# The blocks of a pair's second head in the other half of the partitions, in a chunked delta-rule stage

## The chip, the cores and the metric

The kernel runs on one core of one Trainium2 chip. The metric is the device time of one execution in microseconds (us), from the first instruction to the last; the lower the better.

## The reference

The program is three transformer layers over 512 tokens of width 1024, in float32. The change lies in one part of the last layer, the RWKV-7 mixer, whose core is this recurrence (16 heads of 64 features; everything of one head is a 64 x 64 state):

```python
def wkv7_scan(r, w, k, v, a, b):
    def step(state, inp):
        r_t, w_t, k_t, v_t, a_t, b_t = inp
        sa = jnp.einsum('bhij,bhj->bhi', state, a_t)
        state = (state * w_t[:, :, None, :] + sa[..., None] * b_t[:, :, None, :]
                 + v_t[..., None] * k_t[:, :, None, :])
        y_t = jnp.einsum('bhij,bhj->bhi', state, r_t)
        return state, y_t
```

It is called with a = -kk and b = kk * a, where kk is the normed key. The kernel computes it in 8 chunks of 64 tokens: within a chunk the effect of a on b is a strictly triangular 64 x 64 matrix A, and what is needed is X = (I - A)^-1 and a few products with it. Only what leaves a chunk goes through the 8 chunks in order, in a later stage that the change does not touch.

## The kernel before, in words

The features lie on the 128 partitions, so one tile of 128 features is a pair of heads, head 0 in partitions 0 to 63 and head 1 in 64 to 127. A tile is 128 x 512: 512 tokens, or 8 chunks. The stage runs over the m = 0 to 7 head pairs (KD = 8). Each pair has 16 blocks of 64 x 64 (2 heads e, 8 chunks c).

Every product is written by `products`: 16 matmuls of 64 x 64 with 64 moving columns, in float32. In the records one such matmul is two MATMULs and two LDWEIGHTS, so a product is 32 of each. A 64 x 64 matmul uses one quarter of TensorE's array: the half of the rows is given by the partitions of its operands, the half of the columns by the partitions of its output. There are three layouts. By feature, head e is in partition half e. By token and by chunk, the block (e, c) lies in partition half c % 2, whichever the head. A product from features to chunks (the grams `ab_t`, `ab`, `ak_t`, `rk_t`, `rb_t`) or from chunks to features (`r_new`, `y0`, `m`, `n`) therefore meets all four quarters, and its blocks go out in the order QUADRANTS, four quarters in turn, into the two halves of a pair of PSUM banks. A product from chunks to chunks (`z`, `dx`, `dxt`, `u0`, `a_new`, `akv`) has row half = column half = c % 2: it meets only the two quarters on the diagonal, in the order DIAGONAL.

The four token tiles (`b_tok`, `a_tok`, `k_tok`, `v_tok`) are turned by `turned`: four full 128 x 128 transposes or matmuls for each tile, three with "ident" and one (v) with "centre".

For one pair, the inverse is built in five levels n. At each, PE multiplies `z` = lv X, ScalarE copies z out of PSUM, PE multiplies `dx` = Xt z and `dxt` = z Xt, VectorE adds dx into X (`add`) and dxt into Xt (`addt`), and the next level's z waits for the add. lv is the masked A of the level (VectorE, `level`). What does not belong to this chain is put between by hand. PE's queue for pair m is: z1, the end products of the pair before (`ends_x`: u0, a_new), dx1 and dxt1, z2, `ends_r` (r_new, y0), dx2 and dxt2, `ends_m` (m, n), z3, the token tiles of pair m + 1, dx3 and dxt3, `bonus`, `grams_ab`, z4, `grams_k`, dx4 and dxt4, `gram_rb`, z5, `spread` of pair m + 2, `weighted` (akv) of pair m + 1, dx5. VectorE and ScalarE have orders of their own, written in the same way; `need` is a wait on a step of another engine, `mark` the increment that ends a step. The PSUM banks are given by `bank`: z in 0, dx in 1, dxt in 2, the rest share 3 to 7.

```python
        DIAGONAL = [((c + n) % 2, c) for n in range(2) for c in range(NC)]
        QUADRANTS = [(e, c + (e + n) % 2) for c in range(0, NC, 2) for n in range(2) for e in range(2)]
```

## Time and profile before

| | |
|---|---|
| device time, three runs | 3702.94, 3708.01, 3711.56 us; median 3708.01 us |
| the profiled execution: its own time | 3705.42 us |
| its span in the trace | 3703.0 us |
| granted TensorE clock over the span | 0.953 |
| PE busy | 3418.7 us (92%), 22118 matmuls |
| VectorE busy / ScalarE busy | 1870.1 us (51%) / 1174.5 us (32%) |
| HBM read | 279.33 MB, 76 GB/s over the span |

Times in the trace run from the start of the span. PE is the matmul record, PEld the weight load beside it, DVE is VectorE, ACT ScalarE. PEclk is the granted TensorE clock as a share of full speed. L2583 is the matmul in `products`; the whole stage lies between about 2855 and 3118 us. In a timeline row, `x32` is the number of instructions that are merged into the row, the first two numbers are start and duration of the merged row in us, and what stands in square brackets is how long the engine was idle before it and what ended the idle time; "issue" is a wait for nothing that the profile shows.

### The profile page before, as it was taken

The numbers are of one execution on the slowest core, as the hardware profiler recorded it, in microseconds if no ns is written. First come the engines' busy times: TensorE is split into PE (matmuls) and PEld (weight loads), VectorE is DVE, ScalarE is ACT, GpSimd is POOL, SyncE is SP. The second block draws the span as 40 slices with busy tenths as digits, with TensorE's granted clock in tenths as the row PEclk, the third lists the DMA queues.
The fourth block names the chain that finished last, engine by engine and source line by source line (L and its number), as shares of the span: only waits on it lengthen the run. The fifth ranks groups of instructions, "written<-read, shape, count | busy, mean of one in ns | idle before, by whom it ended". The sixth has DMA issues, their size and how long they took to land. (4 is left out here: it accounts for less than half of the span.)

```text
span 3703.0 us, 50171 instructions
## 1 busy us (share of the span) xinstructions
PE 3418.7 (92%) x22118; PEld 2782.0 (75%) x22118; DVE 1870.1 (51%) x2306; ACT 1174.5 (32%) x1444; POOL 76.8 (2%) x52
## 2 busy tenths in 40 slices
PE   8999998999999999698999979999688888799996
PEld 7777787787878888687888857887476777588884
DVE  5344565776354434553544365443744664654435
ACT  3225544322232223242322243221423332232223
POOL 0000000000000001000100020000000000000001
PEclk9899999999999999799999989999698999899998
DMA  4101122222222223122222312222122000122231
GB/s 164 46 35 36 56 103 80 80 100 87 98 84 99 84 99 124 42 86 97 87 95 89 105 57 91 102 86 75 42 73 78 4 4 14 52 91 96 88 108 39
DMA packets 44279, 284.63 MB, mean 77 GB/s; under 512 B 5152, under 2 KB 5408, under 8 KB 17824
## 3 DMA queue, kind: packets, MB, share of 16 engines
q1 hardware_dynamic: 44064, 281.45, 21.9%
q8 instruction: 174, 2.85, 0.3%
q14 instruction: 41, 0.34, 0.0%
HBM read 279.33 MB, written 2.10 MB: 76 GB/s over the span
## 5 line engine op out<-in xcount | busy, mean ns | idle before, releaser
L440 PE MATMUL ps<-xh,wh 128*128 128x512 f32 x2464 | 981.0, 398 | 88.5 <-DVE xl L854 33.9
L440 PE MATMUL ps<-xl,wh 128*128 128x512 f32 x2464 | 971.7, 394 | 0.0
L440 PE MATMUL ps<-xh,wl 128*128 128x512 f32 x2464 | 970.9, 394 | 0.0
L311 DVE TENSOR_TENSOR wl<-raw,wh 128x2048 fp32r<-128x2048 f32 (+3 forms) x284 | 591.4, 2083 | 440.6 <-ACT wh L306 440.2
L440 PEld LDWEIGHTS ps<-xh,wh 128*128 128x128 f32 x2464 | 468.3, 190 | 222.2 <-issue 104.4
L306 ACT CAST wh<-raw 128x2048 fp32r<-128x2048 f32 (+3 forms) x284 | 492.4, 1734 | 301.4 <-PE ps L440 296.0
L440 PEld LDWEIGHTS ps<-xh,wl 128*128 128x128 f32 x2464 | 468.1, 190 | 102.2 <-issue 2.1
L440 PEld LDWEIGHTS ps<-xl,wh 128*128 128x128 f32 x2464 | 468.7, 190 | 98.2 <-issue 2.2
L440 PE MATMUL ps<-hid_h,wh 128*128 128x512 f32 x880 | 346.8, 394 | 2.7 <-DVE wl L311 2.7
L440 PE MATMUL ps<-hid_l,wh 128*128 128x512 f32 x880 | 345.2, 392 | 0.0
L440 PE MATMUL ps<-hid_h,wl 128*128 128x512 f32 x880 | 343.7, 391 | 0.0
L1768 ACT ACTIVATE tmp<-tmp 128x512 f32<-128x512 f32 x88 | 55.7, 633 | 560.7 <-DVE tmp L1776 560.7
L1776 DVE TENSOR_TENSOR tmp<-ps,rs 128x512 f32<-128x512 f32 x88 | 60.9, 692 | 317.4 <-PE ps L440 308.5
L440 PEld LDWEIGHTS ps<-hid_h,wh 128*128 128x128 f32 x880 | 165.7, 188 | 40.3 <-DVE wl L311 4.1
L440 PEld LDWEIGHTS ps<-hid_h,wl 128*128 128x128 f32 x880 | 165.6, 188 | 37.9
L440 PEld LDWEIGHTS ps<-hid_l,wh 128*128 128x128 f32 x880 | 165.6, 188 | 34.6
L2583 PE MATMUL ps<-x_area 64*64 64x64 f32 x4864 | 140.1, 222 | 20.4 <-issue 14.5
L2583 PEld LDWEIGHTS ps<-x_area 64*64 64x64 f32 x4864 | 131.0, 136 | 34.0 <-issue 25.5
L726 POOL TENSOR_TENSOR h<-tmp,h 128x512 f32<-128x512 f32 x48 | 76.6, 1629 | 3553.5 <-DVE tmp L719 3553.5
L1025 DVE COPY ybuf<-ps 128x512 f32<-128x512 f32 x40 | 27.7, 692 | 181.6 <-PE ps L440 181.5
L1056 ACT ACTIVATE tmp<-ybuf 128x512 f32<-128x512 f32 x40 | 25.3, 632 | 285.4 <-DVE ybuf L1025 220.4
L1761 DVE TENSOR_TENSOR hid_l<-tmp,hid_h 128x512 fp32r<-128x512 f32 x110 | 76.1, 692 | 75.5 <-ACT hid_h L1757 75.5
(363 smaller groups left out, 4166.7 us busy)
## 6 DMA issues: line engine op xcount, KB each, us to landing
raw<-in_up SPq DMA_DIRECT2D x88, 1024.0 KB, 4.8
raw<-in_down SPq DMA_DIRECT2D x64, 704.0 KB, 4.0
raw<-in_up_c SPq DMA_DIRECT2D x22, 1024.0 KB, 4.8
raw<-in_down_c SPq DMA_DIRECT2D x16, 704.0 KB, 4.1
raw<-in_gates SPq DMA_DIRECT2D x8, 1024.0 KB, 4.8
raw<-in_gv SPq DMA_DIRECT2D x8, 1024.0 KB, 5.2
raw<-in_gu SPq DMA_DIRECT2D x8, 1024.0 KB, 4.8
raw<-in_gout SPq DMA_DIRECT2D x8, 1024.0 KB, 4.8
```

Of the source, the lines that this page charges most:

```text
L306: nc.scalar.copy(wh[:, slot, 0:w], raw[:, slot, 0:w]).then_inc(hi_ready, 1)
L311: nc.vector.tensor_tensor(wl[:, slot, 0:w], raw[:, slot, 0:w], wh[:, slot, 0:w].bitcast(F32), ALU.subtract).then_inc(lo_ready, 1)
L440: last = nc.tensor.matmul(out, stationary, moving, start=(fresh and q == 0), stop=(t == kt - 1 and half == per - 1 and q == 2), skip_group ...
L726: nc.gpsimd.tensor_tensor(dst, self.scratch(2 + t % 2), dst, ALU.add).then_inc(n_onto.sem, 1)
L1025: last = (nc.vector.tensor_copy(dst, products[m]) if scale is None else nc.vector.tensor_scalar(dst, products[m], scale, None, ALU.mult))
L1056: nc.scalar.activation(squares(u, m), buf[:, k * blocks + m, tokens], ACT.Square).then_inc(act_steps.sem, 1)
L1761: nc.vector.tensor_tensor(hid_l[:, k, tokens], tmp[:, 2 + u, tokens], hid_h[:, k, tokens].bitcast(F32), ALU.subtract).then_inc(dve_steps.s ...
L1768: nc.scalar.activation(tmp[:, u, :], tmp[:, u, :], ACT.Silu).then_inc(act_steps.sem, 1)
L1776: nc.vector.tensor_tensor(tmp[:, u, :], products[0], rs[:, :], ALU.mult).then_inc(dve_steps.sem, 1)
L2583: last = nc.tensor.matmul(dst, stationary, right(rhs, e, c), start=(n == 0), stop=(n == len(pairs) - 1), skip_group_check=True)
```

## The change

Head 1's blocks move to the other partition half in half of the tiles. `rows_of(e, c, turned)` gives the half: c % 2 as before, or (c + e) % 2 for a turned tile. b, k and v tokens, the masked grams, Xt, z and what the ends produce are turned; X, lv and the a tokens are not. Then

- z, dx, u0, a_new and akv each go from one kind to the other, meet all four quarters, and go out in the order QUADRANTS (13 of the 33 products that a pair now has). dxt stays on the diagonal; r_new, y0, m, n and the grams had four quarters before and keep them.
- the token tiles are no longer turned as 128 x 128 but block by block: 16 matmuls of 64 x 64 for each of the four (`token`, and `products` for v).
- Xt needs A in the turned layout, so the gram `ab` is multiplied a second time, `ab_f` (`gram_again`); VectorE masks it straight out of PSUM (`first_xt`) in place of the copy in SBUF.
- outputs lie in halves of bank pairs, z and dx in the two halves of banks 0 and 1, so z1 now also waits for `add5` of the pair before. `bonus` and `spread` share bank 7.
- ScalarE copies b and a tokens in one instruction, k and v in one, and u0 and a_new in one (128 x 1024 each), after the second of the two is done. The token tiles wait for all readers of their bank pair.
- the queues change: akv moves from before z1 to behind z1, `gram_rb` from before z5 to behind it, `gram_again` and `spread` come behind dx5; on VectorE `bonus` goes before the masks, and `scaled_keys` behind the last of them. `ends_x` waits for `xt0` of the next pair in place of `bonus` and `akv` of the next pair.

```diff
-        bank = {"b_tok": 7, "a_tok": 3, "k_tok": 4, "v_tok": 5, "bonus": 7, "ab_t": (3, 0), "ab": (3, 1), "ak_t": (5, 0),
-                "rk_t": (5, 1), "rb_t": (3, 0), "spread": 5, "akv": 6, "u0": 7, "a_new": 6, "r_new": (3, 0), "y0": (3, 1),
-                "m": (5, 0), "n": (5, 1)}
+        bank = {"b_tok": (3, 0), "a_tok": (3, 1), "k_tok": (5, 0), "v_tok": (5, 1), "ab_t": (3, 0), "ab": (3, 1), "ak_t": (5, 0),
+                "rk_t": (5, 1), "rb_t": (3, 0), "ab_f": (5, 0), "akv": (3, 1), "a_new": (5, 0), "u0": (5, 1), "r_new": (3, 0),
+                "y0": (3, 1), "m": (5, 0), "n": (5, 1), "bonus": 7, "spread": 7}
         for n in range(1, 6):
-            bank[f"z{n}"], bank[f"dx{n}"], bank[f"dxt{n}"] = 0, 1, 2
+            bank[f"z{n}"], bank[f"dx{n}"], bank[f"dxt{n}"] = (0, 0), (0, 1), 2
...
+        def rows_of(e, c, turned):
+
+            at_ = C * ((c + e * turned) % 2)
+            return slice(at_, at_ + C)
...
+        def by_turned(x, e, c):
+            o = (e * (NC // 2) + c // 2) * C
+            return x[rows_of(e, c, 1), o:o + C]
...
             def first_xt(m):
-                need(dve, aA, m, "ab")
+                need(dve, pA, m, "ab_f")
                 if m:
                     need(dve, pB, m - 1, "dx5")
-                mark(nc.vector.tensor_tensor(blocks(xt_), blocks(abs_[m % 2]), every(LEVEL), multiply), vB, "xt0")
+                mark(nc.vector.tensor_tensor(of_heads(xt_), in_halves("ab_f"), every_half(LEVEL), multiply), vB, "xt0")
...
-            def end(m, name, out):
-                need(act, pC, m, name)
-                mark(nc.scalar.copy(out, ps[:, bank[name], :]), aC, name)
+            def ends(m):
+                need(act, pC, m, "u0")
+                mark(nc.scalar.copy(tok_pairs["new"][m % 2].rearrange("p q (e s) -> p q e s", e=2), both("a_new")), aC, "new")
...
-            def products(steps, name, out, *pairs):
+            def products(steps, name, out, *pairs, order=QUADRANTS):
 
-                for e, c in (QUADRANTS if out in (half_chunk, half_feature) else DIAGONAL):
+                for e, c in order:
...
+            def token(name, x, out):
+                for e, c in QUADRANTS:
+                    last = nc.tensor.matmul(out(name, e, c), by_feature(x, e, c), of_head(table("ident"), e, c), start=True,
+                                            stop=True, skip_group_check=True)
                 mark(last, pA, name)
...
+            def gram_again(m):
+                need(pe, vA, m, "rk_t")
+                gram("ab_f", t_a, t_b)
+
             def weighted(m):
-                need(pe, vA, m, "rk_t")
-                products(pA, "akv", whole_token, (by_chunk, ak_ts[m % 2], by_token, v_toks[m % 2]))
+                need(pe, vA, m, "rb_t")
+                products(pA, "akv", half_chunk, (by_turned, ak_ts[m % 2], by_turned, v_toks[m % 2]))
 
             def z(m, n):
                 if n == 1:
                     need(pe, vA, m, "lv1")
+                    if m:
+                        need(pe, vB, m - 1, "add5")
                 else:
                     need(pe, vB, m, f"add{n - 1}")
-                chunk_product(f"z{n}", lv_, xs_[m % 2])
+                products(pB, f"z{n}", half_turned, (by_chunk, lv_, by_chunk, xs_[m % 2]))
...
-                chunk_product(f"dx{n}", xt_, z_)
+                products(pB, f"dx{n}", half_chunk, (by_turned, xt_, by_turned, z_))
                 if n < 5:
-                    chunk_product(f"dxt{n}", z_, xt_)
+                    products(pB, f"dxt{n}", whole_turned, (by_turned, z_, by_turned, xt_), order=DIAGONAL)
 
             def ends_x(m):
                 need(pe, vB, m, "add5")
+                need(pe, aA, m, "akv")
                 if m + 1 < KD:
-                    need(pe, vA, m + 1, "bonus")
-                    need(pe, aA, m + 1, "akv")
-                else:
-                    need(pe, aA, m, "akv")
-                products(pC, "u0", whole_token, (by_chunk, xs_[m % 2], by_token, ak_ts[m % 2]))
-                products(pC, "a_new", whole_token, (by_chunk, xs_[m % 2], by_token, a_toks[m % 2]))
+                    need(pe, vB, m + 1, "xt0")
+                products(pC, "a_new", half_turned, (by_chunk, xs_[m % 2], by_chunk, a_toks[m % 2]))
+                products(pC, "u0", half_turned, (by_chunk, xs_[m % 2], by_chunk, ak_ts[m % 2]))
...
             for m in range(KD):
                 behind, ahead, next_ = m > 0, m + 1 < KD, m + 2 < KD
                 z(m, 1)
+                weighted(m)
                 if behind:
                     ends_x(m - 1)
                 dx(m, 1)
...
                 dx(m, 4)
+                z(m, 5)
                 if ahead:
                     gram_rb(m + 1)
-                z(m, 5)
+                dx(m, 5)
+                if ahead:
+                    gram_again(m + 1)
                 if next_:
                     spread(m + 2)
-                if ahead:
-                    weighted(m + 1)
-                dx(m, 5)
```

## Rows read from the trace of the kernel before

**Rows 1.** The page: PE over the span, and the queue that carries PE's instructions

```profile
PE 3418.7 (92%) x22118; PEld 2782.0 (75%) x22118; DVE 1870.1 (51%) x2306; ACT 1174.5 (32%) x1444; POOL 76.8 (2%) x52
...
q8 instruction: 174, 2.85, 0.3%
```

**Rows 2.** Windows: us, then PE, PEld, DVE, ACT, POOL busy, PEclk, DMA, GB/s

```profile
2868.00:2898.00 30.00, 24.48 (x664) 22.05 (x664) 19.89 (x32) 10.09 (x21) 0.00 (x0) 0.89 0.01 3
2898.00:3056.00 158.00, 137.06 (x4600) 124.00 (x4600) 108.73 (x171) 54.39 (x100) 0.00 (x0) 1.00 0.02 4
3056.00:3086.00 30.00, 26.47 (x921) 24.53 (x918) 20.34 (x33) 8.64 (x16) 0.00 (x0) 1.00 0.02 4
3086.00:3118.00 32.00, 23.92 (x928) 22.82 (x928) 13.42 (x21) 6.84 (x12) 0.00 (x0) 1.00 0.02 4
```

**Rows 3.** Timeline of PE: the `spread` behind pairs 0 and 5

```profile
2893.85 1.12 PE L2618 MATMUL ps<-key_norms,const 32*128 32x512 f32 x2 [1.19 <-DVE spare_l L2385]
...
3052.00 1.12 PE L2618 MATMUL ps<-key_norms,const 32*128 32x512 f32 x2 [1.18 <-DVE x_area L2385]
```

**Rows 4.** Timeline, the bare chain of the last pair: dx3, add3, z4, copy, dx4

```profile
3100.13 2.08 PE L2583 MATMUL ps<-x_area 64*64 64x64 f32 x64 [0.68 <-ACT x_area L2517]
...
3101.33 0.69 DVE L2375 TENSOR_TENSOR spare_l<-ps,spare_l 128x512 f32<-128x512 f32 x1 [0.54 <-PE ps L2583]
...
3102.07 1.15 PE L2583 MATMUL ps<-spare_l,x_area 64*64 64x64 f32 x32
...
3103.27 0.59 ACT L2517 COPY x_area<-ps 128x512 f32<-128x512 f32 x1 [1.85 <-PE ps L2583]
...
3103.91 2.08 PE L2583 MATMUL ps<-x_area 64*64 64x64 f32 x64 [0.69 <-ACT x_area L2517]
```

**Rows 5.** Timeline of PE: bonus and two grams; b, a, k tokens; v tokens

```profile
2979.98 1.12 PE L2647 MATMUL ps<-rs,const 128*128 128x512 f32 x2
2981.03 1.16 PE L2583 MATMUL ps<-x_area 64*64 64x64 f32 x64
...
2974.72 1.53 PE L2609 MATMUL ps<-const,x_area 128*128 128x128 f32 x12
...
2976.90 1.13 PE L2611 MATMUL ps<-const,v 128*128 128x128 f32 x8 [0.66 <-ACT ag L2529]
```

**Rows 6.** Timeline of PE: between two stalls in pair 3

```profile
2969.58 3.01 PE L2583 MATMUL ps<-x_area 64*64 64x64 f32 x128 [0.91 <-issue]
2973.34 0.51 PE L2583 MATMUL ps<-x_area 64*64 64x64 f32 x19 [0.75 <-issue]
```

**Rows 7.** DMA from 2970 to 2974 us, in slices of 0.1 us

```profile
GB/s 0 0 0 0 0 0 164 0 0 0 0 0 0 0 0 0 0 0 0 0 0 0 0 0 0 0 0 0 0 0 0 0 0 0 0 0 0 0 0 0
...
q8 instruction: 1, 0.02, 2.0%
```

**Rows 8.** DMA of the whole stage, 2860 to 3118 us

```profile
q8 instruction: 57, 0.93, 1.6%
```

**Rows 9.** What PE waited for, 2868 to 3118 us: us, times, longest

```profile
PE ps L2583 <- issue: 20.0, 25, 1.5
PE ps L2611 <- ACT ag L2529: 3.4, 6, 0.7
```

**Rows 10.** Timeline of the turn of pair 2 to 3: add5, mask, bonus, ends

```profile
2959.88 0.69 DVE L2375 TENSOR_TENSOR x_area<-ps,x_area 128x512 f32<-128x512 f32 x1 [2.64 <-PE ps L2583]
2960.49 0.68 DVE L2385 TENSOR_TENSOR spare_l<-ps,masks 128x512 f32<-128x512 f32 x1
...
2961.09 0.68 DVE L2389 TENSOR_TENSOR v<-ps,v 128x512 f32<-128x512 f32 x1
...
2961.87 1.32 PE L2583 MATMUL ps<-x_area 64*64 64x64 f32 x38 [1.10 <-issue]
```

**Rows 11.** Windows and PE's timeline where the granted clock is half

```profile
2870.40:2877.20 6.80, 5.38 (x96) 5.22 (x96) 4.48 (x8) 0.58 (x1) 0.00 (x0) 0.50 0.02 4
...
2871.19 5.38 PE L2583 MATMUL ps<-x_area 64*64 64x64 f32 x96 [3.25 <-DVE x_area L2370]
```

More of the change, by code:

```diff
@@ L2211, in rwkv @@
         abs_ = (ab, ab_other)
[L2212 removed]
+        b_toks, a_toks, ak_ts, rk_ts, k_toks, v_toks, rb_ts, xs_ = zip(*sets)
+        tok_pairs = {"b_a": (x_area[:, 8:10, :], spare_h[:, 0:2, :]), "new": (x_area[:, 9:11, :], spare_h[:, 1:3, :]),
+                     "k_v": (x_area[:, 12:14, :], spare_l[:, 0:2, :])}
         reset, masks = area("reset", [P, T], 92 * KB), area("masks", [P, 11, C], 94 * KB)
@@ L2319, in operand_a @@
                 if m:
-                    need(dve, pA, m - 1, "ak_t")
+                    need(dve, pA, m - 1, "ab_f")
                 by, of = blocks(e_kk), blocks(t_a)
@@ L2331, in operand_b @@
                 if m:
-                    need(dve, pA, m - 1, "rb_t")
+                    need(dve, pA, m - 1, "ab_f")
                 mark(nc.vector.tensor_tensor(t_b, e_kk, e_wi, multiply), vL, "b")
@@ L2344, in first_x @@
                 if m >= 2:
-                    need(dve, pC, m - 2, "a_new")
+                    need(dve, pC, m - 2, "u0")
                 x = xs_[m % 2]
@@ L2373, in add_x @@
                 need(dve, pB, m, f"dx{n}")
-                x = xs_[m % 2]
-                mark(nc.vector.tensor_tensor(x, ps[:, bank[f"dx{n}"], :], x, add), vB, f"add{n}")
+                x = in_heads(xs_[m % 2])
+                mark(nc.vector.tensor_tensor(x, in_halves(f"dx{n}", False), x, add), vB, f"add{n}")
             def add_xt(m, n):
@@ L2416, in grams @@
                 with_eye(m)
+                bonus(m)
                 masked(m, "ak_t", ak_ts[m % 2], STRICT, "rk_t")
@@ L2420, in grams @@
                 masked(m, "rb_t", rb_ts[m % 2], UPTO, "rb_t")
-                bonus(m)
             masks_here(dve)
@@ L2493, in decays, with tokens @@
                 mark(nc.scalar.activation(tile(wc, m), e_w[:, C - 1:T:C], ACT.Copy), aE, "wc")
-            def token(m, name, out):
-                need(act, pA, m, name)
+            def tokens(m, name, behind):
+                need(act, pA, m, behind)
                 if m >= 2:
                     need(act, pC, m - 2, "n")
-                mark(nc.scalar.copy(out, ps[:, bank[name], :]), aA, name)
+                out = tok_pairs[name][m % 2].rearrange("p q (e s) -> p q e s", e=2)
+                mark(nc.scalar.copy(out, both("b_tok" if name == "b_a" else "k_tok")), aA, name)
             def lower(m):
@@ L2508, in weighted @@
                 need(act, pA, m, "akv")
-                mark(nc.scalar.copy(ak_ts[m % 2], ps[:, bank["akv"], :]), aA, "akv")
+                mark(nc.scalar.copy(in_heads(ak_ts[m % 2]), in_halves("akv", False)), aA, "akv")
             def z(m, n):
@@ L2549, in _ @@
                 z(m, 1)
+                weighted(m)
                 if behind:
-                    end(m - 1, "u0", ak_ts[(m - 1) % 2])
-                    end(m - 1, "a_new", a_toks[(m - 1) % 2])
+                    ends(m - 1)
                 z(m, 2)
@@ L2559, in _ @@
                 if ahead:
-                    tokens(m + 1)
+                    tokens(m + 1, "b_a", "a_tok")
+                    tokens(m + 1, "k_v", "v_tok")
                 z(m, 4)
@@ L2568, in _ @@
                     decays(m + 2)
-                if ahead:
-                    weighted(m + 1)
-            end(KD - 1, "u0", ak_ts[(KD - 1) % 2])
-            end(KD - 1, "a_new", a_toks[(KD - 1) % 2])
+            ends(KD - 1)
             answer(KD - 1)
@@ L2615, in spread @@
                 if m:
-                    need(pe, vA, m - 1, "rk_t")
+                    need(pe, vA, m - 1, "bonus")
                 rows = slice(32 * (m % 4), 32 * (m % 4) + 32)
@@ L2693, in ends_x @@
-                products(pC, "u0", whole_token, (by_chunk, xs_[m % 2], by_token, ak_ts[m % 2]))
-                products(pC, "a_new", whole_token, (by_chunk, xs_[m % 2], by_token, a_toks[m % 2]))
-            def ends_r(m):
-                need(pe, aC, m, "a_new")
-                if m + 1 < KD:
-                    need(pe, vA, m + 1, "rb_t")
-                products(pC, "r_new", half_feature, (by_token, a_toks[m % 2], by_chunk, rb_ts[m % 2]))
-                products(pC, "y0", half_feature, (by_token, ak_ts[m % 2], by_chunk, rb_ts[m % 2]),
-                         (by_token, v_toks[m % 2], by_chunk, rk_ts[m % 2]))
@@ new lines, in ends_x, with ends_r @@
+                products(pC, "u0", half_turned, (by_chunk, xs_[m % 2], by_chunk, ak_ts[m % 2]))
+            def ends_r(m):
+                need(pe, aC, m, "new")
+                if m + 1 < KD:
+                    need(pe, aA, m + 1, "akv")
+                products(pC, "r_new", half_feature, (by_turned, a_toks[m % 2], by_turned, rb_ts[m % 2]))
+                products(pC, "y0", half_feature, (by_turned, ak_ts[m % 2], by_turned, rb_ts[m % 2]),
+                         (by_turned, v_toks[m % 2], by_turned, rk_ts[m % 2]))
@@ L2724, in _ @@
             gram_rb(0)
+            gram_again(0)
             spread(1)
-            weighted(0)
             for m in range(KD):
```

117 lines of the change are left out of this document (47 added, 70 removed).

## The prediction

> **What bounds the kernel now.** I read the page first: PE 92% busy, the other engines far below [rows 1]. Only the stage of the head pairs changes, so I went on to the windows of that stage. Pairs 1 to 5 issue 4600 matmuls in 158 us, 920 a pair, and PE counts as busy for 137 of them, VectorE for 109, ScalarE for 54 [rows 2]. The spread, once a pair, gives the period: (3052.00 - 2893.85) / 5 = 31.63 us [rows 3]. The stage ends in the states that the next one begins with, so what it gains or loses the kernel does too.
>
> Then the timeline, for what a product costs. On two quarters, 64 matmuls (dx and dxt) take 2.08 us [rows 4]; the last 0.22 us of a row is the modelled end of the last matmul, so that is 0.93 us a product, 29 ns a matmul. On four quarters, 64 matmuls of two grams take 1.16 us [rows 5], 0.47 us a product, 14.6 ns a matmul. So a product of two quarters that moves to four is done in 0.46 us less. The bare chain runs dx3, add, z4, copy, dx4 in 3.78 us a level [rows 4].
>
> Last, PE's idle time. 20.0 us in the stage, 25 times, are put down to "issue" [rows 9]. The stall at 2973.34 begins in the middle of a product, where the code waits for nothing. Between the end of the stall before it and this one lie exactly 128 matmuls, with their loads 256 instructions [rows 6]. The queue q8 carries PE's instructions: 44236 matmuls and loads on 174 packets are 254 a packet [rows 1]. The packet between the two stalls starts at 2970.6, 1.0 us after PE went on at 2969.58, takes 2.0% of 16 x 4 us = 1.3 us, and PE goes on 1.4 us after its end [rows 6, 7]. So I read: when PE enters a block of 256 instructions, the next one is asked for, and it is there 1.0 us, the packet and 1.4 us later. Over the stage a packet takes 1.6% x 16 x 258 / 57 = 1.16 us [rows 8]. **No 256 instructions can then go by in less than about 3.6 us**, which is 28 ns a matmul with its load: hardly less than what a product on two quarters takes anyway, and twice what one on four takes.
>
> The Trainium skill, "Runtime: NRT & Kernel Launch", section "Instruction fetch mechanics", says that instructions come in blocks of 16 KiB (256 instructions) fetched while the current one runs, and that the cost of crossing into the next is mostly hidden. The trace agrees with the block and differs on the cost.
>
> **The change, part by part.**
> 1. z, dx, u0, a_new and akv, 13 products: 13 x 0.46 = 6.0 us of matmul time less a pair.
> 2. `ab_f`: 0.47 us and 32 matmuls more.
> 3. Token tiles: 12 + 8 matmuls in 1.53 + 1.13 us [rows 5], about 2.2 us without the tails, become 4 x 32 matmuls in 4 x 0.47 = 1.9 us: no gain worth the name, but 108 matmuls more.
> 4. Together 6 us less to do, in 920 - 20 + 32 + 128 = 1060 matmuls: 2120 instructions and some 35 waits, 2155 for 256 a block, 8.4 blocks. At 3.6 us they take **30.3 us**. Before, 1840 + 35 are 7.3 blocks, 26.4 us, under a period of 31.63: the supply only showed as single stalls. After, it sets the pace.
> 5. Waits. I walked the new queues through one pair as if instructions were always there, with 0.47 and 0.93 us for products, 0.27 us from the start of a product's last matmul to its reader (z4's at 3102.07 + 1.15 - 0.22 = 3103.00, the copy at 3103.27 [rows 4]), 0.6 us from one VectorE start to the next [rows 10], 0.69 and 0.59 us for an add and a copy [rows 4], 1.0 us for a copy of 1024 (an estimate, twice the 0.59 less its fixed part), 1.1 us for bonus and for spread [rows 3, 5]. A whole pair comes to about 25 us. The slow place is its turn. From the end of dx4, VectorE does add4, addt4, bonus, two masks and lv1 before add5 (ends at 4.9 us), then the rb mask, k2, rkr and xt0 (ends at 7.4), for which `ends_x` waits; `gram_again` waits for the rk mask (3.75), spread ends at 5.3, a_new can start at 7.45 and dx1 at 8.4 us. That lies beside 290 matmuls, 8.3 us of supply: they cover each other but for some 0.3 us.
> 6. Tokens wait for y0, n and their banks: 2.3 us from dxt2's or z3's end, beside 64 to 128 matmuls (1.8 to 3.6 us of supply), hidden but for a few tenths at worst. The larger ScalarE copies lie beside PE work. ScalarE and VectorE get no more to do.
> 7. Removed: `ends_x` no longer waits for `bonus`, which ends at 2961.77 and lets PE idle 1.1 us [rows 10]; the wait for `xt0` (point 5) takes its place. The v tokens' wait for n, 3.4 us in the stage [rows 9], becomes that of point 6. In the new pace both are time in which the next block arrives.
>
> **The sum.** Pairs 1 to 5: 30.3 + 0.3 = 30.6 against 31.6, 5 x 1.0 = 5 us less. Pair 6: no spread, 30.3 against 29.7 (its z1 to the next): 0.6 us more. Pair 0 has no ends, 804 matmuls or 23 us of supply, and took 30 us, at half clock for 6.8 us of them, when 96 matmuls on two quarters took 5.4 us [rows 11]; there the chain sets the time. dx1 to dx3 becomes about 2.5 us shorter (z2, dx2, z3 and the tokens' order), dx3 to the next z1 1.1 us (452 matmuls of supply, 12.9 us, against 14.0), the start 0.5 us (two grams wait for two copies, not four): 4 us less. The last pair: up to dx3, 512 matmuls of supply, 14.6 us against 15.5: 0.7 less. From there five products at 0.46 on the bare chain [rows 4] and u0 and a_new, 3.2 us, less 0.4 for the copy of both: 3 us less, since 448 matmuls of supply (12.8 us) still go under 13 of 16. Sum: -5 + 0.6 - 4 - 0.7 - 3 = -12 us. The profiled execution took 3705.4 us, the median of the runs shown is 2.6 us above it: 3708.0 - 12 = 3696. Small losses where supply and chain fall out of step are likelier than further gains, so I say **3697 us**, its own range 3690 to 3704.
>
> **The rivals.**
> - *The supply is no limit* (0.06). Then the walk of point 5 holds: 25 us a pair against 31.6 is 5 x 6.6 us, some 5 more in pair 6 and 14 in the first and last together, 52 us: 3656 us. This is what the page named above would make of it. Against it stand the stall in mid-product [rows 6] and 25 waits for "issue" [rows 9].
> - *No measurable change* (0.23). Supply and chain don't overlap at the turn of a pair: a block that arrives late there delays addt4 and with it the VectorE row up to xt0. At 1 us a pair the gain of pairs 1 to 5 is gone, 3701 us; if the same happens in pairs 0, 6 and 7, up to 3709 us. For it speaks that at the turn both need 8.3 us, so each slip adds.
> - *Slower, the four quarters do not run side by side* (0.07). In the new z, dx, r_new, y0, m and n, the two row halves write into the same bank of the pair at the same time; in today's four-quarter products each row half keeps its bank. If that costs them the pace, all 33 products take 0.93 us: 30.7 + 2.2 + the waits of the turn, about 35.5 us a pair, +3.9 x 7: 3735 us. It decides only from about 25 ns a matmul, since up to there the supply is slower. Against it: today's two-quarter products have both row halves in one bank and run at 58 ns for each quarter, as the four-quarter ones do (4 x 14.6). The Trainium skill, "TensorEngine Tiling (Array Packing)", section "Restrictions and Gotchas", says that different row tiles cannot access one PSUM bank at the same time. By that rule this rival would hold; the trace of the diagonal does not show it.
> - *Slower, the clock* (0.04). PE now works in bursts with stalls between. If the granted clock fell to half for half of the stage, as in [rows 11], where matmuls took twice as long, a pair would take about 39 us (29 products at 0.93, dxt at 1.87, bonus and spread at 2.2): +7 x 4 = 28 us: 3736 us. Against it: 1.00 from 2898 on, through stalls of over 1 us [rows 2, 6].
> - *The forecast* has the rest, 0.60.
>
> A measurement of this kernel can tell about 0.2%, 7.4 us, from no change. Of the forecast's 0.60 some 0.54 lies below 3700.6: with the first rival, faster 0.60. Within 0.2%: 0.06 + 0.22 = 0.28. Slower: 0.11 and 0.01 of the second rival, 0.12. The range leaves out the first rival and the two slow ones: 3686 (nothing lost anywhere, all 67 blocks of the stage at 3.6 us: 242 us against 262) to 3709.
>
> **What would show it.** Right: q8 packets in the stage up from 57 to about 66, one every 3.6 us; most of PE's idle time put down to "issue", far over 20 us; z and dx as rows of 32 in 0.47 + 0.22 us where no stall cuts them; a spread every 30.6 us; VectorE and ScalarE as busy as before; clock 1.00. Wrong: a period of 27 us or less (supply no limit), matmuls of z at 29 ns (quarters), waits of PE on VectorE over 1 us a pair at `ends_x` (turn), PEclk under 1 in pairs 1 to 6.

## The result, and the profile after

| | before | after |
|---|---|---|
| median of 20 runs | 3705.97 us (3702.13 to 3712.06) | **3719.19 us** (3704.45 to 3729.52) |
| mean granted clock over those runs | 0.951 | 0.9465 |
| the profiled execution: its own time, span, clock | 3705.42, 3703.0 us, 0.953 | 3710.82, 3708.4 us, 0.949 |

The changed kernel takes 1.0031 of the time of before (95% interval 1.0021 to 1.0040): some 11.5 us slower, where 12 us faster was forecast. (The ratio goes by the means, 3706.90 and 3718.31 us; the medians are 13.2 us apart.) The profiled execution of after is one of its quicker ones, so the profile shows less than half of the difference: something varies from run to run.

The page of after, PE over the span and its instruction queue, which answers to [rows 1]:

```profile
PE 3407.5 (92%) x23238; PEld 2769.5 (75%) x23238; DVE 1869.7 (50%) x2306; ACT 1172.0 (32%) x1420; POOL 76.8 (2%) x52
...
q8 instruction: 183, 3.00, 0.3%
```

There are 1120 more matmuls and nine more packets of instructions, as the change asks for; yet PE is busy for 11 us less, and the kernel is slower.

Windows of after, one for each head pair (columns as in [rows 2]):

```profile
2863.00:2893.00 30.00, 25.91 (x826) 23.55 (x824) 20.68 (x34) 9.26 (x17) 0.00 (x0) 0.73 0.02 4
2893.00:2925.00 32.00, 24.99 (x1065) 21.98 (x1060) 21.63 (x34) 10.61 (x17) 0.00 (x0) 1.00 0.02 4
2925.00:2957.00 32.00, 26.21 (x1060) 23.44 (x1051) 21.63 (x35) 10.61 (x17) 0.00 (x0) 0.95 0.02 4
2957.00:2994.00 37.00, 29.12 (x1070) 25.60 (x1063) 21.56 (x35) 10.67 (x17) 0.00 (x0) 0.86 0.02 4
2994.00:3025.00 31.00, 24.66 (x1059) 21.84 (x1055) 21.43 (x35) 10.60 (x17) 0.00 (x0) 1.00 0.02 5
3025.00:3058.00 33.00, 26.71 (x1087) 23.96 (x1088) 22.47 (x36) 10.61 (x17) 0.00 (x0) 0.95 0.02 4
3058.00:3092.00 34.00, 26.97 (x1072) 24.38 (x1074) 19.86 (x33) 8.25 (x12) 0.00 (x0) 0.90 0.02 4
3092.00:3122.00 30.00, 22.29 (x943) 20.95 (x939) 11.69 (x18) 7.17 (x11) 0.00 (x0) 0.94 0.02 4
```

The column to read is PEclk. Before, it stood at 1.00 from 2898 us on [rows 2]; now six of eight windows are below it. Added up over the clock's records from the first `z1` to the last `n`, the granted clock was half for 43.6 us, against 6.8 us before [rows 11]. Some 16 us of the 43.6 lie in pair 0, in one stretch of 17.1 us that begins at 2862.0. Where the clock stayed full, in pairs 1 and 4, a pair takes 32.1 and 31.2 us. That is no less than before and 0.6 to 1.5 us more than forecast. From the end of one pair's `z1` to the end of the next one's, in us:

| | 0 | 1 | 2 | 3 | 4 | 5 | 6 | 7 | stage | at half clock |
|---|---|---|---|---|---|---|---|---|---|---|
| before | 30.0 | 31.1 | 31.8 | 31.8 | 31.3 | 32.2 | 29.7 | 31.6 | 249.4 | 6.8 |
| after | 29.9 | 32.1 | 32.4 | 36.9 | 31.2 | 33.1 | 33.4 | 30.5 | 259.5 | 43.6 |
| e1, below | 27.1 | 30.7 | 31.6 | 31.3 | 30.7 | 33.2 | 29.9 | 27.9 | 242.4 | 19.7 |

The last row is of e1, the first experiment below. So there are two things to explain: why a pair at full clock gained nothing, and why the clock fell.

**A product at one quarter's pace.** VectorE's adds show how far `dx` and `dxt` of one level end apart. The timeline of VectorE in after, add3 (L2391) and addt3 (L2395) of pair 4:

```profile
3012.34 0.69 DVE L2391 TENSOR_TENSOR x_area<-ps,x_area 128x512 f32<-128x512 f32 x1 [2.85 <-PE ps L2591]
3013.90 0.69 DVE L2395 TENSOR_TENSOR x_area<-ps,x_area 128x512 f32<-128x512 f32 x1 [0.87 <-PE ps L2591]
```

They start 1.56 us apart; the working had 0.93 us for `dxt`. By PE's own records it is 1.64 us in the median, 32 matmuls at 51 ns. The reason can be read in the code. DIAGONAL takes e = (c + n) % 2. The blocks of the second head now lie turned, in row half (c + e) % 2, and for e = (c + n) % 2 that is n for every c. The output lies in the same half, so the first eight blocks all use one quarter of the array, and the other eight use another. Two quarters are used, but one after the other. (The matmuls of a product with both row halves in one bank do keep the four-quarter pace: a_new and u0 below.)

Timeline of PE in after, a_new and u0, and the b and a tokens:

```profile
2995.85 1.16 PE L2591 MATMUL ps<-spare_h,spare_l 64*64 64x64 f32 x64 [1.04 <-DVE x_area L2384]
...
3007.95 1.15 PE L2615 MATMUL ps<-const,x_area 64*64 64x64 f32 x64
```

64 matmuls in 1.16 us are 0.47 us a product, as the two grams of [rows 5]. The four quarters do run side by side.

**Instructions.** Timeline of PE in after, last pair, three stalls in a row:

```profile
3098.75 2.71 PE L2591 MATMUL ps<-x_area 64*64 64x64 f32 x128 [0.83 <-issue]
3102.37 2.36 PE L2591 MATMUL ps<-x_area 64*64 64x64 f32 x107 [0.91 <-issue]
3105.84 0.46 PE L2591 MATMUL ps<-spare_l,x_area 64*64 64x64 f32 x15 [0.75 <-issue]
```

PE goes on at 3098.75, 3102.37 and 3105.84, 3.62 and 3.47 us apart, and the first of these stretches is exactly 128 matmuls: 256 instructions with their loads. This is the supply of [rows 6]. One thing has to be added to the working. In after's stage no instruction packet on q8 starts sooner than 3.28 us behind the one before it, and in the stage of none of the other profiles is that distance under 3.2 us. But 128 matmuls in a row that begin in the middle of a block can be quicker: at full clock, two of pair 1's grams and what follows them in pair 0's queue do it in 2.10 us, the last one's end included:

```profile
2882.71 2.10 PE L2591 MATMUL ps<-x_area 64*64 64x64 f32 x128
```

So the limit is from one block to the next; a stretch that begins in the middle of a block isn't bound by it. The DMA of the stage in after (2863 to 3122 us), and what PE waited for in it:

```profile
q8 instruction: 63, 1.03, 1.7%
```

```profile
PE ps L2591 <- issue: 27.7, 29, 2.2
PE ps L2591 <- DVE x_area L2384: 5.2, 6, 1.0
PE ps L2615 <- ACT ag L2545: 4.7, 4, 1.2
```

63 packets in 259 us are one every 4.1 us. The supply limits in places, but over the stage it is not used up: the waits for `xt0` (L2384), which sit at `ends_x` of six pairs, and the slow `dxt` (e13 below) leave it idle.

**The clock.** Windows of after, before and behind one of the falls, and PE's timeline there:

```profile
2974.70:2978.10 3.40, 1.21 (x82) 1.06 (x75) 0.00 (x0) 1.83 (x2) 0.00 (x0) 0.99 0.02 5
2978.10:2984.90 6.80, 6.80 (x95) 5.18 (x98) 2.61 (x3) 0.00 (x0) 0.00 (x0) 0.50 0.01 2
```

```profile
2974.82 0.68 PE L2591 MATMUL ps<-const,v 64*64 64x64 f32 x32
2975.29 0.56 PE L2591 MATMUL ps<-x_area 64*64 64x64 f32 x23
2978.04 3.52 PE L2591 MATMUL ps<-x_area 64*64 64x64 f32 x41 [2.19 <-issue]
2981.49 2.07 PE L2645 MATMUL ps<-rs,const 128*128 128x512 f32 x2
```

PE had 1.21 us of work in the 3.4 us before 2978.10, with a stall of 2.19 us in the middle of a product. Behind it the clock is at half, 1.2 GHz, for 6.8 us, in which 95 matmuls keep PE busy without a gap and `bonus` takes 2.07 us instead of 1.12. The falls in the stage don't all look like this one. There are eight, and the longest idle time of PE in the 5 us before each was, in order:

| fall at, us | 2862.0 | 2926.9 | 2964.4 | 2978.1 | 3036.1 | 3063.4 | 3080.5 | 3118.0 |
|---|---|---|---|---|---|---|---|---|
| idle before, us | 1.1 | 1.0 | 2.2 | 2.2 | 1.6 | 1.9 | 1.9 | 1.1 |
| then at half clock, us | 17.1 | 3.4 | 3.4 | 6.8 | 3.4 | 3.4 | 3.4 | 3.4 |

No single stall of a given length goes with a fall. In e1's profile a stall of 1.85 us at 3028.1 is followed by 19 us at full clock. Before `spread`, PE waits 1.2 us for VectorE in the kernel before, six times, and the clock stays full (two of them in [rows 3]); behind the same wait it fell three times in the profiled execution of e12, four times in e2 and three times in e3 (the experiments below). What decides it is not shown here.

### The profile page after: what moved, and what is told of

Same layout as the page of the kernel before. It is cut to its first block and busy times, and to the rows that moved or that the text cites. A ratio compares the mean times of both kernels' runs of the same rounds, so it can differ in the third digit from the quotient of the medians.

```text
span 3708.4 us, 52376 instructions
## 1 busy us (share of the span) xinstructions
PE 3407.5 (92%) x23238; PEld 2769.5 (75%) x23238; DVE 1869.7 (50%) x2306; ACT 1172.0 (32%) x1420; POOL 76.8 (2%) x52
## 5 line engine op out<-in xcount | busy, mean ns | idle before, releaser
L1025 DVE COPY ybuf<-ps 128x512 f32<-128x512 f32 x40 | 27.7, 692 | 179.9 <-PE ps L440 179.8
```

The lines of the kernel that those rows point to most:

```text
L1025: last = (nc.vector.tensor_copy(dst, products[m]) if scale is None else nc.vector.tensor_scalar(dst, products[m], scale, None, ALU.mult))
```

## The experiments

Ratios are to runs of the kernel before that were taken beside the experiment's, with their 95% interval; where two experiments are compared, it is by these ratios. "Clock" is the mean granted clock of a kernel's runs.

### e1: the order of dxt alone

```
+        BY_HEAD = [(e, c) for e in range(2) for c in range(NC)]
...
-    products(pB, f"dxt{n}", whole_turned, (by_turned, z_, by_turned, xt_), order=DIAGONAL)
+    products(pB, f"dxt{n}", whole_turned, (by_turned, z_, by_turned, xt_), order=BY_HEAD)
```

> The changed kernel with one thing altered: dxt goes out head by head, so that its 16 blocks alternate between the two diagonal quarters; in the changed kernel the order DIAGONAL with turned blocks sends eight in a row to one quarter (1.64 us a dxt in its trace, against 0.93 before). Theory A (the order of dxt is the loss, and the half-clock windows follow from work on one quarter): dxt back to 0.93 us, no more half-clock windows inside the stage than before, a pair about 30.6 us, device time some 10 us under the kernel before. Rival B (the clock falls because PE works in bursts between instruction stalls): dxt at 0.93 us, but the granted clock still falls to half several times in the stage and the time stays within 5 us of the changed kernel. Rival C (the supply of instructions hides dxt's order): no change of the period at full clock, 31.2 us.

Measured: 3700.94 us, **0.9989 (0.9977 to 1.0001)**, clock 0.950. VectorE in e1, add3 and addt3 of one pair:

```profile
3007.82 0.69 DVE L2392 TENSOR_TENSOR x_area<-ps,x_area 128x512 f32<-128x512 f32 x1 [2.85 <-PE ps L2592]
3008.76 0.69 DVE L2396 TENSOR_TENSOR x_area<-ps,x_area 128x512 f32<-128x512 f32 x1 [0.24 <-PE ps L2592]
```

0.94 us apart. Windows of e1 (pair 2, most of pair 4, pair 5):

```profile
2927.00:2958.00 31.00, 22.83 (x1056) 19.67 (x1047) 22.18 (x35) 10.61 (x17) 0.00 (x0) 1.00 0.02 4
2990.00:3020.00 30.00, 21.82 (x1025) 19.07 (x1020) 21.20 (x34) 10.53 (x17) 0.00 (x0) 1.00 0.02 4
3020.00:3054.00 34.00, 25.47 (x1108) 21.78 (x1112) 24.44 (x39) 10.68 (x18) 0.00 (x0) 0.93 0.02 5
```

Its instruction packets and PE's waits for "issue" in the stage:

```profile
q8 instruction: 64, 1.05, 1.8%
```

```profile
PE ps L2592 <- issue: 40.0, 36, 2.2
```

One line of issue order is worth 0.42% between after and e1, 16 us. Of pairs 1 to 5, those at full clock throughout are 4 with 30.7 us and 2 with 31.6 (forecast 30.6); a packet comes every 3.8 us, and 40 us of idle time go to "issue". With the order that the forecast had assumed, the forecast's picture is there in the main, but its 12 us are not: 4 us, with no change at the edge of the interval. The stage of the profiled run is 7 us shorter than before. Neither theory A nor rival B holds as it was put down. `dxt` is back at 0.93 us, but the clock still falls four times, 19.7 us of the stage against 6.8 before; and the time is 16 us under after's, not within 5. Rival C falls by the time; the few pairs at full clock (30.7 and 31.6 us, in after 31.2 and 32.1) would not have decided it.

### e2: the kernel before with dxt on one quarter at a time

```
+        BY_HALF = [(e, c) for h in range(2) for e in range(2) for c in range(h, NC, 2)]
...
-                    chunk_product(f"dxt{n}", z_, xt_)
+                    products(pB, f"dxt{n}", whole_chunk, (by_chunk, z_, by_chunk, xt_), order=BY_HALF)
```

> The kernel before with dxt alone in the changed kernel's order: the eight blocks of one partition half, then the eight of the other. Theory A: dxt 1.64 us in place of 0.93, z behind it late by about 0.6 us four times a pair, some 15 to 20 us more in all, and half-clock windows in the stage if one quarter at work is what lowers the clock. Rival B: +15 us at the most from the products themselves and the clock stays at 1.00 in pairs 1 to 6, since the supply of instructions is as slack as before.

Measured: 3730.93 us, **1.0058 (1.0044 to 1.0071)**, clock 0.950. `dxt` takes 1.68 us; four in a pair are 4 x 0.75 x 8 = 24 us more, and 21.5 came. The clock has a share in this: it is 0.950 against 0.9515 for before, and in the profiled execution it falls to half four times between 2900 and 3037 us, each time behind the wait for VectorE before `spread`. At equal clock (below) some 18 us are left. So in the kernel before, `dxt` lies on the path with about three quarters of its length.

### e8, e13: two quarters again, with dxt in either order

e8 is e1 with z, dx, akv, a_new and u0 head by head, which was meant to let two quarters run side by side, not four; e13 is e8 with dxt in DIAGONAL again.

```
-                products(pB, f"z{n}", half_turned, (by_chunk, lv_, by_chunk, xs_[m % 2]))
+                products(pB, f"z{n}", half_turned, (by_chunk, lv_, by_chunk, xs_[m % 2]), order=BY_HEAD)
...
```

> The kernel with dxt alternating, and z, dx, u0, a_new and akv (13 products a pair) in the order head by head, which uses two quarters at a time: everything of the new layout is kept, only the four quarters are given up. Each of the 13 takes 0.93 us again, 6.0 us more matmul time a pair. If the supply of instructions sets the pace (3.6 us for 128 matmuls, 28 ns each, hardly less than the 29 of two quarters): 0.5 to 1.5 us a pair, 3705 to 3713 us, and the clock lowered less often, since PE works more evenly. If PE's own time or the chain sets it: 4 to 6 us a pair, 3730 to 3750 us.

> The changed kernel with its 13 four-quarter products in the order head by head (two quarters at a time) and dxt as in the changed kernel (one quarter at a time): the fourth of a square whose others are the changed kernel, dxt alternating, and two quarters with dxt alternating. If dxt's order costs the same with and without the four quarters: 3719 to 3722 us. If the four quarters are what lowers the clock, since PE then stands idle between blocks: less than the changed kernel, 3712 to 3717 us, with a mean granted clock above its 0.9465.

Measured, e8: 3703.34 us, **0.9992 (0.9979 to 1.0006)**, clock 0.952. e13: 3707.17 us, **0.9995 (0.9985 to 1.0006)**, clock 0.951. Together with after and e1 this is a square:

| | dxt on one quarter | dxt on two |
|---|---|---|
| 13 products on four quarters | 1.0031 (after) | 0.9989 (e1) |
| 13 products on two quarters | 0.9995 (e13) | 0.9992 (e8) |

The label "two quarters" is only nearly right. Head by head, these products meet two quarters with their first eight blocks and the other two with the last eight, and the halves overlap. Timeline of PE in e13, dx5 of the last pair:

```profile
3113.01 0.97 PE L2592 MATMUL ps<-x_area 64*64 64x64 f32 x32 [0.69 <-ACT x_area L2534]
```

Without the 0.22 us at its end that is 0.76 us, where a product in the kernel before takes 0.93 [rows 4]; two in a row (z1 and akv, a_new and u0) take 1.35 us in both e8 and e13. So the 13 products cost 0.2 to 0.3 us each, 2.6 to 3.6 us a pair and 21 to 29 us in all, and not the 48 us of the expectation.

The lower row of the table: with the products on two quarters dxt's order costs 1 us, which is within the intervals, and the upper row: with four it costs 16 us. Read by columns: the four quarters, which do these 21 to 29 us less of matmul time, give 1 us in the one case and take 13 us in the other. Where they went shows in the stages of the profiled executions. From e1 (2868.16 to 3111.54 us) to e8 (2868.97 to 3116.82) PE's busy time is up from 179.5 to 196.9 us, and its idle time down from 63.8 to 50.9: three quarters of the additional busy time went into time in which PE had stood idle. Timeline of PE in e8:

```profile
3033.26 2.78 PE L2592 MATMUL ps<-x_area 64*64 64x64 f32 x128 [1.11 <-issue]
3036.73 0.57 PE L2592 MATMUL ps<-x_area 64*64 64x64 f32 x19 [0.69 <-issue]
```

Even here PE goes on at 3033.26 and 3036.73, 3.47 us apart.

In e13 the same goes for `dxt`. PE's waits for "issue", in e8 and then in e13:

```profile
PE ps L2592 <- issue: 30.6, 34, 1.7
```

```profile
PE ps L2592 <- issue: 14.4, 18, 1.5
```

The slower `dxt` has filled 16 us of the time in which the next block was on its way. In e2 it filled less: "issue" is 10.7 us there, against 20.0 in before [rows 9], and `dxt` cost 18 to 21 us. This fits, but no run tests it; the turned kernel has another order of tokens and ends as well. And it doesn't say why the same order costs 16 us with the four quarters, where the profiles have even more idle time. The mean clocks do differ there: 0.9465 (after) and 0.9498 (e1) with four quarters, 0.9509 (e13) and 0.9518 (e8) with two. Both orders of `dxt` have the lower clock with four quarters, and four quarters with `dxt` on one have by far the lowest.

### e3, e4: more matmuls in the kernel before

```
             def gram(name, left, right):
+                if name in ('ab_t', 'ab', 'ak_t', 'rk_t'):
+                    for e, c in QUADRANTS:
+                        nc.tensor.matmul(half_chunk(name, e, c), by_feature(left, e, c), by_feature(right, e, c), start=True,
+                                         stop=True, skip_group_check=True)
```

e4 repeats only ab_t and ak_t, and takes the added ones in DIAGONAL.

> The kernel before with four grams (ab_t, ab, ak_t, rk_t) issued twice in the order of the four quarters: 128 matmuls a pair more, 1.9 us of PE time, one block of 256 instructions. By the supply of instructions (3.6 us for 256): 8.3 blocks a pair, 30 us at least, and more stalls: 2.5 to 3.5 us a pair, 20 to 28 us in all, and clearly more than the run with two grams twice. If the supply is no limit: 1.9 us a pair at most, 15 us, and the same as that run.

> The kernel before with two grams (ab_t, ak_t) issued twice, the added ones on two quarters at a time: 64 matmuls a pair more, 1.9 us of PE time as in the run with four grams twice, but half a block of instructions. By the supply: 28 us a pair, so still under the period, and only the PE time counts: about 12 to 15 us in all. If the supply is no limit: the same as the run with four grams twice.

Measured, e3: 3736.62 us, **1.0075 (1.0062 to 1.0089)**, clock 0.952. e4: 3717.07 us, **1.0029 (1.0015 to 1.0043)**, clock 0.952. In e3 the added matmuls would take 4 x 0.47 = 1.9 us a pair at their pace, 15 us in all; 0.75% are 28 us, 3.5 us a pair. That is what one block of 256 instructions costs at the pace of the stalls (3.5 to 3.6 us). e4 was meant to add the same matmul time, but it doesn't: its added products overlap their halves too, and ab_t's takes 0.70 us in e4's trace (from the first matmul to the next product's), not 0.93. So e4 adds about 1.4 us a pair, 11 us, and cost 11 us: its matmul time and no more. With 64 more matmuls a pair, e3 costs 13 us more than its matmul time. That speaks for a price of the instructions themselves, without any quarter being changed. The profiled execution of e3 shows only part of it as idle time: the stage (2865.23 to 3140.71 us) is 24.0 us longer than before's (2865.85 to 3117.31), with PE busy for 18.4 us more and idle for 5.7 us more, and some 7 us more of it are at half clock.

### e6: e1 without the second gram

```
             def gram_again(m):
-                gram("ab_f", t_a, t_b)
+                e, c = QUADRANTS[-1]
+                mark(nc.tensor.matmul(half_turned("ab_f", e, c), by_feature(t_a, e, c), by_feature(t_b, e, c), start=True,
+                                      stop=True, skip_group_check=True), pA, "ab_f")
...
-  mark(nc.vector.tensor_tensor(of_heads(xt_), in_halves("ab_f"), every_half(LEVEL), multiply), vB, "xt0")
+  mark(nc.vector.tensor_tensor(blocks(xt_), blocks(abs_[m % 2]), every(LEVEL), multiply), vB, "xt0")
```

> The kernel with dxt alternating, and the second gram (ab_f) left out but for its last block, so that 30 matmuls a pair fall away; Xt is masked from the copy of ab in SBUF, so the blocks of head 1 in it are in the wrong half and the output is not the reference's. By the supply of instructions: 60 instructions fewer, 8.2 blocks a pair, 29.5 us, 0.8 us a pair or about 6 us under the kernel with dxt alternating (3700.9), and fewer half-clock windows. If the supply is no limit and the chain at the turn of a pair sets the time: nothing or 0.5 us a pair at most.

Measured: 3703.76 us, **0.9995 (0.9985 to 1.0006)**, clock 0.948. 30 matmul records less a pair (60 of 2155 instructions, a quarter of a block) gave nothing that is measured. "Fewer half-clock windows" was wrong: the granted clock is lower than e1's, and in the profiled execution about 41 us of the stage are at half, against e1's 19.7. Its time at equal clock is in the account below.

### e9: fewer instructions, but mixed shapes

e1 with the first head's token tiles as four matmuls of 64x128, beside eight of 64x64 for the second head: 44 calls a pair for the four token tiles instead of 64, each call two matmul records:

```
+                for n in range(TB):
+                    last = nc.tensor.matmul(ps[:, b, o:o + HD], x[0:HD, n * P:(n + 1) * P], of_head(onto, 0, 0), start=True, ...)
+                    if turned:
+                        for c in (2 * n, 2 * n + 1):
+                            last = nc.tensor.matmul(half_turned(name, 1, c), by_feature(x, 1, c), of_head(onto, 1, c), start=True, ...)
```

> The kernel with dxt alternating, and the token tiles made with fewer matmuls where the layout allows it: two chunks of a head in one matmul of 128 stationary columns for head 0 of all four tiles and head 1 of a; 44 matmuls in place of 64, so 40 recorded matmuls or 80 instructions a pair fewer, 0.3 block. By the supply: 1.1 us a pair, some 8 us under the kernel with dxt alternating, 3693 us, and the best version so far. If the supply is no limit: within 2 us of it, or slower by what the mixed shapes cost.

Measured: 3773.46 us, **1.0182 (1.0164 to 1.0200)**, clock 0.940. Timeline of PE in e9, the b tokens at full clock:

```profile
3012.67 0.43 PE L2621 MATMUL ps<-const,x_area 64*128 64x64 f32 x2
3013.03 0.33 PE L2625 MATMUL ps<-const,x_area 64*64 64x64 f32 x4
3013.29 0.43 PE L2621 MATMUL ps<-const,x_area 64*128 64x64 f32 x2
```

Six records take 3013.29 - 3012.67 = 0.62 us, against 6 x 14.6 ns = 0.09 us for 64x64 alone; with two changes of shape in each group some 0.2 us a change remain, an estimate (the wider matmul's own time is not known). Three tiles with eight changes each are 24 x 0.2 = 5 us a pair, 38 us in all; the rest of the 72 us above e1 comes with a clock lower by 0.010. The stage has eight falls in e9's profile. Before most of them PE counts as busy without a gap, but with few matmuls, here before a fall and behind it (columns as in [rows 2]):

```profile
2940.20:2943.61 3.41, 3.41 (x43) 2.87 (x44) 0.00 (x0) 1.01 (x1) 0.00 (x0) 1.00 0.03 7
2943.61:2950.44 6.83, 6.83 (x93) 5.89 (x92) 0.69 (x1) 1.01 (x1) 0.00 (x0) 0.50 0.00 0
```

So the clock falls without any stall as well. Nothing about the supply can be learnt from e9, since the shapes cost more.

### e10, e11, e12: room on PE, and the turn of the pair

e10 is e1, and e11 the kernel before, with `bonus` issued three times (4 matmuls of 128x512 and some 2.1 us of PE time more in each pair, 8 instructions):

```
+                for _ in range(2):
+                    nc.tensor.matmul(ps[:, bank["bonus"], :], table("heads"), e_sum, start=True, stop=True)
```

e12 is the kernel before with another order of VectorE's queue: `bonus` ahead of the masks of the grams, `scaled_keys` behind the last mask.

```
+                    bonus(m + 1)
                     masked(m + 1, "ak_t", ak_ts[(m + 1) % 2], STRICT, "rk_t")
...
                     masked(m + 1, "rb_t", rb_ts[(m + 1) % 2], UPTO, "rb_t")
-                    bonus(m + 1)
                 if next_:
+                    scaled_keys(m + 2)
                     bonus_terms(m + 2)
```

> The kernel with dxt alternating, and the bonus matmul (128x512, all of the array) issued three times in place of once, with the same result: 2.1 us more PE time a pair, but 8 instructions. If the supply of instructions sets the pace, PE has room: under 0.7 us a pair, within 5 us of the kernel with dxt alternating (3701), and, if the clock falls because PE has too little to do between blocks of instructions, a higher mean granted clock than its 0.950 and then even no more time. If PE's time or the chain sets it: 2 us a pair, 15 us more.

> The kernel before with the same two added matmuls of 128x512 a pair. Its period of 31.6 us is not set by the supply (26.4 us) but by PE's queue with its waits: 1.5 to 2.1 us a pair, 11 to 16 us more. If its PE had as much room as the supply theory says of the changed kernel: nothing.

> The kernel before with one part of the change alone: VectorE's queue of the changed kernel at the turn of a pair (bonus ahead of the masks, scaled keys behind them), so that the end products no longer wait for the bonus (1.1 us a pair). Layout, products and instructions as before. The supply allows 26.4 us a pair, so the wait is really gained: 0.7 to 1.1 us a pair, 5 to 8 us in all, 3698 to 3702 us, as good as the changed kernel with dxt alternating. Rival: the stall only moves to the next block of instructions or to xt, and nothing is gained.

Measured, e10: 3708.25 us, **1.0002 (0.9992 to 1.0011)**, clock 0.951. e11: 3727.19 us, **1.0044 (1.0028 to 1.0060)**, clock 0.951. e12: 3705.55 us, **0.9991 (0.9980 to 1.0001)**, clock 0.951. The same 17 us of PE time with hardly an instruction in it cost the kernel before 16 us, nearly all, and e1 about 5 us (1.0002 against 0.9989). In e1, PE time between dxt3 and the grams is largely covered; before, it is on the path. Part of e10's small price is the clock, as its expectation had it: 0.951 against e1's 0.950, and in the profiled execution one fall behind pair 0 where e1 has three. At equal clock (below) the 17 us cost 8 us. e12 missed its 5 to 8 us. It shows that the part of the change that has nothing to do with quarters, `ends_x` no longer behind `bonus`, can be had alone, and its ratio stands where e1's does. What PE waited for in the stage of e12:

```profile
PE ps L2582 <- issue: 9.5, 19, 1.1
PE ps L2582 <- DVE x_area L2370: 7.9, 7, 1.3
```

"Issue" is down from 20.0 us [rows 9], and waiting for VectorE at L2370, one wait of 3.3 us before, is up to 7.9: most of the gain went there, as the rival had it. Neither e1 nor e12 is shown to beat the kernel before: both intervals reach 1.0001.

### The time at equal clock

The runs of one kernel differ in granted clock, and their times follow it. After's run at 0.950 took 3704.45 us and one at 0.944 took 3729.52. The clock is on record to 0.001 only, so what follows is rough. A straight line through the runs of each kernel in the table falls by 1.7 to 3.4 us for 0.001 of clock, and gives at 0.950:

| | before | after | e1 | e8 | e13 | e6 |
|---|---|---|---|---|---|---|
| mean clock | 0.951 to 0.952 | 0.9465 | 0.9498 | 0.9518 | 0.9509 | 0.9479 |
| us at 0.950 | 3711 to 3712 | 3706 | 3703 | 3709 | 3710 | 3701 |

At equal clock after is 5 us quicker than before, e1 8 us, e6 11 us, and the four quarters bring 6 us with dxt on two quarters and 4 us with dxt on one. At the clock that each kernel is granted nothing of that is left. Measured from before to after: -5 at equal clock, then 0.005 of clock at about 3 us for 0.001, +15; the sum, +10, is near the 11.5 us measured. The same way e2 comes to 3729 and e10 to 3711. This is an account from many runs and not an experiment, for no kernel here changed the clock alone.

## Why the prediction was wrong

- **The step that failed, first: point 5's 0.93 us for `dxt`.** That price is one of two quarters side by side. The order DIAGONAL on turned blocks takes them one behind the other, 1.64 us. The row halves of `by_turned` and DIAGONAL both stood in the diff; I carried the price over from [rows 4] by the name of the order, and never listed which quarter each of the 16 blocks falls on. e1 shows this to be 16 us of the 24 between the forecast's -12 and the measured +11.5. How the 16 us come about is only in part known. The longer `dxt` alone is about 0.7 us, 32 times, or 21 us. With the products on two quarters the same order costs 1 us (e13 against e8), so it is the order together with the four quarters that costs. By the account at equal clock e1 and after are 3 us apart and the rest goes with the clock; in the profiled stages, 17.1 us apart, after has 23.9 us more at half clock, which is worth 12 us at the most.
- **The step that failed, second: the rival of the clock at 0.04**, with "1.00 from 2898 on, through stalls of over 1 us" against it. It is what happened, though not at the rival's size: not half of the stage, but 43.6 us of 259.5 at half, 36.8 us more than before. At twice the time for what ran there, that is worth at most 18 us, and about 15 by the account at equal clock, where the rival had 28. The argument against it was drawn from one execution. The kernel before has the same clock of 1.00 behind waits of 1.2 us there, but in its variants e2, e3 and e12 the clock fell behind the same waits. With four quarters the mean clock is lower (0.9465 against 0.9509 and, hardly clear of the spread between runs, 0.9498 against 0.9518); that this comes of PE having less to do between blocks is only argued. For it speak the fall behind 2.2 us of stall and that e10, with more work for PE, has a slightly higher clock than e1. But e1 has more "issue" than after (40.0 against 27.7 us) and the higher clock, so idle time alone does not explain after's, and the cause stays open. I had counted "late instructions" and "clock" as two cases with separate chances; here both came together.
- **Point 4, the supply: right as a lower bound, its period a little short.** Stalls 3.5 to 3.6 us apart, 128 matmuls between them; 63 packets where about 66 were forecast; 21 to 29 us of matmul time removed by the four quarters bring 1 us (e8 against e1); e3 costs 13 us more than its matmul time. But the pairs at full clock take 30.7, 31.2, 31.6 and 32.1 us in e1 and after, 0.1 to 1.5 us over the 30.6, so the 0.3 us for the waits at the turn was too little. The Trainium skill, "Runtime: NRT & Kernel Launch", section "Instruction fetch mechanics", has this crossing as mostly hidden. For matmuls as short as these the measurements decide against it: 40.0 us in e1's stage in 36 waits, 1.1 us a time and 2.2 at the longest.
- **Points 1 and 3, the pace of four quarters: right.** 64 matmuls in 1.16 and 1.15 us. So the rival that the four quarters do not run side by side falls. The Trainium skill, "TensorEngine Tiling (Array Packing)", section "Restrictions and Gotchas", forbids two row tiles one PSUM bank at a time; a_new and u0 have both row halves in one bank, at different column halves, and keep 0.47 us a product. One product did run at one quarter's pace, for the reason above and not for this one.
- **Points 5 and 7, the turn.** The wait for `xt0` took the place of that for `bonus` and shows as 5.2 us on VectorE L2384, six times, under the 1 us a pair that would have spoken for the second rival. With the old wait removed alone, e12 comes to 0.9991 where e1 as a whole has 0.9989; neither is clear of no change.
- **The sum, even with dxt mended.** e1's profiled stage is 7.0 us shorter than before's, forecast 12. The last pair gave 3.7 us, as forecast (0.7 + 3); pair 0 gave 2.9 instead of 4, pair 6 lost 0.2 instead of 0.6. Pairs 1 to 5 together gave 0.7 us instead of 5: the two at full clock took 30.7 and 31.6 us, and the other three have some 13 us at half clock. This part failed in the supply's 30.6 us and in the clock, not in `dxt`.
- **"What would make it wrong"** had named PEclk under 1 in pairs 1 to 6. That line did show it.

## What to carry to other kernels

When blocks move in the array, write out for every product the list of quarters in issue order: a price of "two quarters" holds only while neighbours in the queue are on different ones. Count instructions and not only matmul time. Where matmuls are so short that 256 instructions take less than about 3.5 us of work, making them quicker turned mostly into stalls here. And when a change makes an engine burstier, price the granted clock together with the stalls, and look at it in many runs: one profiled execution at full clock doesn't show that a variant of the kernel will keep it.

## What the runs showed of the hardware

- **Instructions.** From one block of 256 instructions to the next PE needs about 3.5 us: stalls 3.47 to 3.62 us apart in after and e8, and no two instruction packets closer than 3.2 us in the stage of any profile. The matmuls of a product on four quarters need half of that time.
- **Quarters.** A 64x64 matmul of float32 with 64 columns takes 51 to 53 ns on one quarter, 29 ns on two taken in turn and 14.6 ns on four. Eight blocks on two quarters and then eight on the other two overlap: 0.76 us a product in e13, against 0.93 before. The order of issue decides which it is.
- **The clock** fell to half in after behind idle times of 1.0 to 2.2 us, and at 2978.1 stayed there for 6.8 us although PE was then busy throughout. In e9 it fell with no idle time before it. Over the runs of one kernel its mean varied by up to 0.009, and the time with it, by up to 25 us.
- **Shapes.** Changing between 64x128 and 64x64 costs about 0.2 us each time, an estimate from e9's rows; e9, with 24 changes a pair, is 67 us slower than before.
